# Who scales the first attention map: a small operation of the differential units goes from VectorE to ScalarE

## The reference, cut to what matters

```python
s = einsum('bqhmd,bkhmd->bhmqk', qb, ka) * (A_DH ** -0.5)      # m = 0, 1: two maps
s = s - slopes * abs(tq[:, None] - pos[None, :])
p = softmax(where(visible, s, -inf), axis=-1)
w = p[:, :, 0] - lam * p[:, :, 1]
out = einsum('bhqk,bkhd->bqhd', w, va)
```

## Time and profile before

| | |
|---|---|
| median of 3 runs | 1342.43 us (1340.15 to 1342.68) |
| the profiled execution, whole | 1342.14 us |
| its span in the trace | 1340.2 us |
| TensorE matmul busy | 1294.9 us, 97% |
| VectorE busy | 871.3 us, 65% |
| ScalarE busy | 565.2 us, 42% |
| GpSimd busy | 477.1 us, 36% |

### The profile page before, as it was taken

How to read it: one execution, slowest core, us unless ns; L and a number is a source line. 1 busy time by engine, 2 the same in 40 slices (tenths; PEclk the granted TensorE clock), 3 DMA queues, 4 the chain that set the end, 5 groups by cost and what they waited for, 6 DMA issues and landing times.

```text
span 1340.2 us, 22174 instructions
## 1 busy us (share of the span) xinstructions
PE 1294.9 (97%) x8228; PEld 1221.5 (91%) x8228; DVE 871.3 (65%) x1959; ACT 565.2 (42%) x1332; POOL 477.1 (36%) x461
## 2 busy tenths in 40 slices
PE   8999999999999999998999999998999999999997
PEld 7999998999899999997888999998999989998886
DVE  5685868586677848669555323654778677776455
ACT  3444646364744535356101012533565545656200
POOL 3323221233224142246533324563333234334531
PEclk9999999999999999998999999999999999999999
DMA  6001010101010111214233311122111112115242
GB/s 227 33 28 36 17 49 32 49 33 48 33 40 25 37 45 52 63 29 137 68 126 126 111 32 61 66 83 75 36 48 45 48 44 64 41 46 194 69 161 79
DMA packets 46922, 88.25 MB, mean 66 GB/s; under 512 B 4048, under 2 KB 29648, under 8 KB 46688
## 3 DMA queue, kind: packets, MB, share of 16 engines
q1 hardware_dynamic: 44368, 78.45, 17.8%
q10 hardware_dynamic: 2448, 8.39, 1.6%
HBM read 66.84 MB, written 19.98 MB: 65 GB/s over the span
## 4 chain that ended last, share of the span: by engine, by line
PE 82%; DVE 9%; ACT 5%; issue 2%; POOL 1%; DMA 1%; DVEq 0%; SPq 0%; ACTq 0%; POOLq 0%
PE bank L2023 41%; PE bank L2174 13%; PE bank L2091 11%; PE bank L2146 8%; PE bank L2113 6%; DVE ring L1808 2%; DVE pb L1790 1%; PE bank L2062 1%; PE bank L2131 1%; ACT rtmp L1390 1%; DVE big L1607 1%; PE bank L2196 1%; DVE big L1847 1%; DVE tb L1737 1%; ACT vtok L1426 1%
## 5 line engine op out<-in xcount | busy, mean ns | idle before, releaser
L2023 PE MATMUL bank<-big,wsp 128*128 128x344 f32 (+2 forms) x3024 | 550.4, 327 | 8.4 <-DVE big L1607 4.5
L2023 PEld LDWEIGHTS bank<-big,wsp 128*128 128x128 f32 x3024 | 481.1, 189 | 15.0 <-POOL wsp L1067 4.2
L1066 POOL TENSOR_SCALAR wsp<-wraw 128x1024 fp32r<-128x1024 f32 (+4 forms) x92 | 84.3, 917 | 529.7 <-PE bank L2023 414.9
L1808 DVE TENSOR_TENSOR ring<-bank,ring 128x512 fp32r<-128x512 f32 (+3 forms) x280 | 154.9, 569 | 71.6 <-ACT ring L1477 44.8
L2174 PE MATMUL bank<-big,wsp 128*128 128x512 f32 x800 | 191.5, 397 | 1.5 <-DVE big L1847 1.2
L2174 PEld LDWEIGHTS bank<-big,wsp 128*128 128x128 f32 x800 | 149.3, 188 | 36.4 <-DVE big L1847 1.7
L1067 POOL TENSOR_TENSOR wsp<-wraw,wsp 128x1024 fp32r<-128x1024 f32 (+4 forms) x92 | 179.3, 1949 | 7.7
L2023 PE MATMUL bank<-h1t,wsp 128*128 128x344 f32 (+2 forms) x1080 | 173.9, 322 | 1.4 <-DVE lraw L1655 1.4
L2023 PEld LDWEIGHTS bank<-h1t,wsp 128*128 128x128 f32 x1080 | 170.2, 188 | 3.6 <-DVE lraw L1655 1.7
L1477 ACT ACTIVATE ring<-bank 128x512 fp32r<-128x512 f32 (+1 forms) x200 | 106.0, 555 | 112.8 <-PE bank L2113 80.4
L2146 PE MATMUL bank<-ring,vtok 128*128 128x256 f32 (+1 forms) x1040 | 143.3, 279 | 2.0 <-DVE ring L1808 1.0
(11 more groups left out here) (138 smaller groups left out, 1497.6 us busy)
## 6 DMA issues: line engine op xcount, KB each, us to landing
wraw<-in_w SPq DMA_DIRECT2D x47, 512.0 KB, 3.4
wraw<-y_scratch SPq DMA_DIRECT2D x17, 448.0 KB, 3.8
woraw<-in_wo SPq DMA_DIRECT2D x12, 512.0 KB, 5.3
y_scratch<-ot SPq DMA_DIRECT2D x37, 128.0 KB, 1.7
xres<-in_x SPq DMA_DIRECT2D x8, 512.0 KB, 4.7
h_scratch<-res ACTq DMA_DIRECT2D x8, 512.0 KB, 2.6
gate_scratch<-gtmp SPq DMA_DIRECT2D x8, 512.0 KB, 2.9
gate<-gate_scratch SPq DMA_DIRECT2D x8, 512.0 KB, 3.7
```

The source lines that it names most:

```text
L1066: pool.wait_ge(S["pool_step"], tick(nc.gpsimd.tensor_scalar(hi, raw, 1.0, 1.0, ALU.mult, ALU.mult)))
L1808: V.tensor_tensor(to, bank[T_BANK[t]][from_, 0:w], lo_hi(R[from_, r % NRING, 0, 0:w]), ALU.subtract)\
L2023: ins = mm(dst, wsp[:, SLOT[kind, u], a, k, :], rhs[:, b, k0 + k, c0:c0 + w], start=(k == 0 and a == 0 and b == 0), stop=last)
```

## The change

C of an A block is cut in three. VectorE first makes both reciprocals and the multiplied one (step I, function `invert_sums`); ScalarE scales the first map by the reciprocal, read as one value for each row, into `pb` (step N, `scaled_map`, an activation of kind Copy); VectorE then only adds the second map (step C). There are two new semaphores, I to N and N to C. ScalarE now also waits until the buffer of `pb` is free, which VectorE did before. In the planner, the one cost becomes three, and N gets the second rank on ScalarE, ahead of the exponentials, the norms and the copies of the projections. The changed costs enter the plan of all of layer 0.

```diff
-RANK = {"pe": "SXTVp", "act": "TSEYQPW", "dve": "PTSMCYFWO", "pool": "CDGQVWO", "sp": "FLO"}
+RANK = {"pe": "SXTVp", "act": "TCSEYQPW", "dve": "PTSMCYFWO", "pool": "CDGQVWO", "sp": "FLO"}
...
-                L.put("dve", "C", ("C", t), 1.9 * n_all + 1000, [("act", ("E", t, 1)), emptied(g)], 90)
+                L.put("dve", "C", ("I", t), 260, [("act", ("E", t, 1))], 90)
+                L.put("act", "C", ("N", t), 0.84 * n_all + 72, [("dve", ("I", t)), emptied(g)], 100)
+                L.put("dve", "C", ("C", t), 1.3 * n_all + 150, [("act", ("N", t)), emptied(g)], 90)
...
+            def scaled_map(t):
+
+                g, i, slot = TSTEPS[t]
+                n = keys_of(i)
+                p_free(act, g)
+                act.wait_ge(S["sums_inverted"], INVERTED[t])
+                A(weights_of(0, slice(0, 128), g, slot, 0, n), tb[:, t % 2, 0, 0:n], ACT.Copy,
+                  scale=stat[:, t % 4, 12:13]).then_inc(S["p_scaled"], 1)
...
+            def invert_sums(t):
+
+                st_ = lambda a, b: stat[:, t % 4, a:b]
+                dve.wait_ge(S["exp_done"], MAPS_DONE[t, 1])
+                then(V.reciprocal(st_(12, 14), st_(8, 10)))
+                V.tensor_scalar(st_(14, 15), st_(13, 14), small[:, 59:60], None, ALU.mult).then_inc(S["sums_inverted"], 1)
...
                 if kind == "A":
-                    dve.wait_ge(S["exp_done"], MAPS_DONE[t, 1])
-                    then(V.reciprocal(st_(12, 14), st_(8, 10)))
-                    V.tensor_scalar(P[:, 0:n], tb[0:rows, t % 2, 0, 0:n], st_(12, 13), None, ALU.mult)
-                    then(V.tensor_scalar(st_(14, 15), st_(13, 14), small[0:rows, 59:60], None, ALU.mult))
+                    dve.wait_ge(S["p_scaled"], SCALED[t])
                     V.scalar_tensor_tensor(out=P[:, 0:n], in0=tb[0:rows, t % 2, 1, 0:n], scalar=st_(14, 15), in1=P[:, 0:n],
                                            op0=ALU.mult, op1=ALU.add).then_inc(S["p_ready_dve"], 1)
```

More of the change, by code:

```diff
@@ L665 @@
 S_FREED = [S_OWNER[:n + 1].count(S_OWNER[n]) for n in range(len(S_OWNER))]
+SCALED = {s[1]: n + 1 for n, s in enumerate(s for s in ORDER["act"] if s[0] == "N")}
+INVERTED = {s[1]: n + 1 for n, s in enumerate(s for s in ORDER["dve"] if s[0] == "I")}
 MAPS_DONE = {}
@@ L856, in trunk_kernel @@
             wo_in_0 wo_in_1 wo_in_2 wo_in_3 wo_in_4 wo_in_5 wo_in_6 wo_in_7 proj_done proj_hi proj_evac proj_read rotated rms_log rms_inverse q_copied lat_sq lat_add lat_sum lat_root lat_norm lat_split
-            s_done s_free_dve s_free_act max_ready exp_done inverted v_cleared v_stepped y_gated p_ready_dve p_ready_pool
+            s_done s_free_dve s_free_act max_ready exp_done sums_inverted p_scaled inverted v_cleared v_stepped y_gated p_ready_dve p_ready_pool
             tr_done tr_hi tr_lo pv_done o_tmp o_evac sq_done unit_done y_stored_0 y_stored_1
@@ L1549, in _ @@
                     exps(*s[1:])
+                elif s[0] == "N":
+                    scaled_map(s[1])
                 elif s[0] == "T":
@@ L1957, in _ @@
                     maxima(*s[1:])
+                elif s[0] == "I":
+                    invert_sums(s[1])
                 elif s[0] == "C":
```

## The result

The changed kernel takes 1352.55 us (median of 4 runs, 1352.13 to 1353.09), the kernel before beside it 1342.56 (4 runs, 1340.15 to 1343.51). The ratio is 1.0082, 95% interval [1.0069, 1.0094]: slower by 10 us by these medians and by 11 by the ratio, outside the predicted range of 1336.5 to 1347.5. The profiled execution took 1352.47 us, with a span of 1350.7.

The account below looks back on a forecast made before the run. The prediction took TensorE to bound the kernel, matmuls busy 97% of the span, with 6.75 us idle in the A units. It summed +0.8 - 1.3 - 1.1 + 0.9 = -0.7 us to 1341.7 us, range 1336.5 to 1347.5.

Parts of the forecast that it names:

- The cost of N, and no table loads: ScalarE, A units: 36 added activations take 26.2 us (23.5 to 29), with no further table loads.
- What TensorE pays for the longer way to w, +0.8: A units: exponentials to w takes 0.42 us longer, charged at 2 of 16 groups; +0.8 us, bounds 0 and 6.7.
- The remark that the plan's margin was gone: Planned way to w at 656 keys: 2.19 us allowed where 2.24 are expected, so the 0.4 us margin goes.
- The wait at 76 to 80, -1.3: TensorE's wait for an addition held beside GpSimd goes entirely: -1.3 us, bounds -1.3 and 0.
- The wait at 52 to 56: TensorE's wait there stays, the addition again falling behind GpSimd's line 1067: 0, possibly -1.2 or +0.3 us.
- VectorE's other waits, -1.1: A units: TensorE's waits for the v copy and score bank, 2.3 us together, halve: -1.1 us, bounds -2.3 and 0.
- The norms on ScalarE, +0.9, at most +5.3: Three norms in the A units: one N in all pushes a logarithm back, +0.9 us; bounds 0 and +5.3.
- The rest of layer 0, 0 with ±3: B units: the plan changes there but nothing in the work does; counted 0, bounds -3 and +3 us.
- What would have shown it wrong: More waits for w, over 2 us for the logarithm, B-unit idle time differing beyond 3 us, or another slow-clock length.
- The range: Whole kernel: 1336.5 to 1347.5 us, from the faster rival with some of the B units to most of the slower.
- The slower one: Rival: ScalarE becomes late where TensorE needs it, N ahead of the norms and w just in time; +5.0, 1347.4 us, chance 0.26.
- It moves work that nobody waits for: Rival: VectorE just waits at C for N, bursts stay as long: 1342.4 us; shares the forecast's chance of 0.43.

Follow-up runs that it names:

- e1: The changed kernel with every engine's order kept, but the first map's scaling left on VectorE and step N empty: 1352.33 us, ratio 1.0083.
- h1: The changed kernel with only the planned cost of C raised from 1.3n + 150 to 1.9n + 740 ns, scaling on ScalarE: 1340.3 us, ratio 1.0003.
- k3: The changed kernel with C planned at 1.9n + 740 ns and the scaling put back on VectorE, N empty: 1340.93 us, ratio 1.0001.
- e4: The changed kernel with N's planned cost raised by 400 ns to 0.84n + 472, VectorE's costs left: 1344.11 us, ratio 1.0025.
- q1: The changed kernel with third logarithm, inverse root and third v copy of units 1 to 3 put ahead of the last block's steps: 1347.32 us, ratio 1.0048.
- e2: The kernel before with its orders kept and the scaling moved to ScalarE, N put where the old plan has C begin: 1357.0 us, ratio 1.0118.
- n1: The kernel before in all its orders, with the first map left unscaled and the norm dividing its sum out: 1336.92 us, ratio 0.9973.
- q2: The changed kernel with GpSimd's copy of the first B unit's third q chunk put ahead of a weight preparation: 1351.01 us, ratio 1.0074.

## Why the prediction was wrong, point by point

The step that failed is the one that gave the new order no price. Every term of the sum took an instruction's effect in the order of before, and the rest of layer 0 was counted as 0. In its place the runs showed that the order alone costs all of the loss (e1: 1352.33 us with the scaling left on VectorE) and that the moved work costs nothing in an order planned for it (h1 against k3).

- *The cost of N, and no table loads:* right. 26.2 us were said; in the A units ScalarE's groups of the changed kernel (count, busy us and mean ns, idle before) show 26.3, and as many loads as before:

```profile
L1464 ACT ACTIVATE tb<-tb,stat 128x16 f32<-128x16 f32 (+8 forms) x72 | 52.4, 729 | 29.2 <-DVE stat L1776 21.4 <-DVE stat L1779 7.5
L1478 ACT ACTIVATE pb<-tb,stat 128x16 f32<-128x16 f32 (+8 forms) x36 | 26.3, 730 | 16.3 <-DVE stat L1786 16.3
L1406 ACT ACT_TABLE_LOAD x6 | 7.7, 1283 | 0.1
```

- *What TensorE pays for the longer way to w, +0.8:* too small. Two groups in 16 were charged 0.42 us; six waits came, 6.1 us in all, 3.6 more than before. N was late by its place, behind an exponential of the next block, and in three of the six the addition was then held beside GpSimd's line 1071 as well. The remark that the plan's margin was gone pointed at the mechanism (e4: 0.4 us more for N in the plan is worth 7.6 us) and was then priced as latency.
- *The wait at 76 to 80, -1.3:* gone as said. *The wait at 52 to 56:* said to stay, all but gone as well (TensorE 3.84 and 4.00 of 4 us), but the same meeting of the 272-key addition with GpSimd came back in units 1 to 3, 0.9 us each. Early on the moved work did gain: from 45 to 100 us TensorE idles 0.2 us in the changed kernel and 2.5 in e1, which has the same order (windows, changed kernel and e1). The later units give it back.

```profile
52.00:56.00 4.00, 3.84 (x27) 3.30 (x25) 3.76 (x17) 3.05 (x9) 2.58 (x3) 1.00 0.40 133
76.00:80.00 4.00, 4.00 (x30) 3.82 (x29) 3.96 (x12) 1.58 (x3) 1.08 (x1) 1.00 0.44 128
45.00:100.00 55.00, 54.83 (x371) 52.99 (x370) 40.05 (x135) 33.35 (x71) 14.20 (x10) 1.00 0.10 31
```
```profile
45.00:100.00 55.00, 52.50 (x352) 50.24 (x351) 43.84 (x137) 25.80 (x60) 14.11 (x10) 1.00 0.09 30
```

- *VectorE's other waits, -1.1:* the score bank's wait went, the copy's stayed at 1.1 us. -1.2, near enough, and covered by what follows.
- *The norms on ScalarE, +0.9, at most +5.3:* the wait was +3.7 us, at all three norms. The step assumed ScalarE's order of before with N put into it. In fact the third logarithm changed sides with the last block's exponentials, and the third v copy with C; the two together are 4.6 us (q1). The bound of two N's a norm counted the wrong instructions.
- *The rest of layer 0, 0 with ±3:* the passage to the B units lost 2.9 us of TensorE's busy time by the windows, and part of it ran at the lower clock. Here the failed step is in plain words: "nothing in the work of that part changes" was true and no reason, as e1 shows.
- *What would have shown it wrong* named the order last, by an idle time in the B units that differs by over 3 us. It differs by 2.8 (11.1 of 300 against 8.3), all of it in the passage, so that sign would have missed it; more waits for w, and over 2 us for the logarithm, both came. The kernel's plan was described as reordering all of layer 0, and the sum was then made as if the order stood still.
- *The range.* Its working says that the terms reach from about -4.5 to +5. Their own upper bounds, 6.7 for w, 5.3 for the norms and 3 for the rest, add up to +15, and with the wait at 52 to 56 to +15.3; no step leads from there to +5. The measured +10 lies within the bounds and outside the range.
- *The rivals.* The slower one had two right places, the logarithm and w just in time, and a wrong cause. By its cause, the loss should have gone with the scaling back on VectorE; in e1 it stays. "It moves work that nobody waits for" was right about the work (twice zero) and wrong about the change. The Trainium skill's rule that multiplications go to VectorE ("ScalarE: Activation LUTs", section "Rules for kernel authors") found no support in time: with the scaling on VectorE and on ScalarE the one order gave 1352.33 and 1352.55 us, the other 1340.93 and 1340.3.

## What to carry to other kernels

Where a planner orders the engines, a change is two changes, its work and its plan; run each alone before pricing either. Here the work was worth 0 in two orders planned with a place for it, and cost 16 us when it was put into the old one (e2); the plan alone was worth 8 to 20 us of 1340. A truthful cost is no better than a padded one by itself: try the planned costs as knobs, and after every change of them look for waits that come once a unit, since these are the order's. Work taken away altogether, in an order that is kept, gave more than work moved (n1, -4 us).

## What the runs showed of the hardware

- TensorE's clock: behind a wait of 2.55 us the changed kernel ran a stretch at a mean granted 0.79, with eight matmuls in 3.19 us instead of 1.93; h1, with a wait of 2.6 us in the same passage, kept 1.00, and q2 had 0.79 with no wait there over 1.2 us. Such a wait is thus neither enough nor needed; what decides is open.
- An addition of VectorE over 272 keys took 1.51 us and ended 0.30 us behind a GpSimd instruction that ran when it began; for 400 keys with none beside it, it took 0.63.
- A Copy on ScalarE with a scale read per row costs what an exponential of that width does: 730 ns in the mean against 729, 0.29 us at 16 keys and 1.17 at 1040.
